# A large attention, pooling and retention kernel: modulation sums, their weight loads and the first operand splits get other places in the plan, and a transpose pair becomes a matmul pair

## The chip, the cores and the metric

The kernel runs on one core of a Trainium2 chip. The metric is the device time of one execution in microseconds (us). Engines are named as in the profile: PE (matmul) with PEld (its weight loads), DVE (vector), ACT (scalar), POOL, and SP, which here only starts transfers.

## The reference

Everything is float32, 512 tokens of width 2048, with 256 context tokens. Three layers follow each other:

```python
# layer 1: attention           layer 2: pooling             layer 3: second block
m = silu(c) @ mod_w + b        # 2048 x 6144; shift, scale, gate (also for c_ctx in layer 1)
h = rmsnorm(x) * (1 + scale) + shift
proj = h @ w_in
y = mix(proj) * silu(z)        # heads 0-7 dense, 8-15 banded | pooling | stick-breaking, retention
x = x + gate * rmsnorm(y @ w_out)      # layer 3 without this norm
```

The "modulation" is the vector-matrix product `silu(c) @ mod_w`. Only its first part in layer 1 (shift and scale, needed for `h` at once) is made in a prologue; the layer-1 gate and all of layers 2 and 3 are made beside the large products.

## The kernel before

**One plan for all engines.** `make_plan` (L311) writes a list of stages. Each engine's program walks through the same list in order and issues its own part of each stage; between engines there are semaphores only. So the place of a stage in the list is its place in the queue of every engine that takes part in it.

**Chunks.** All large weights come in chunks of 512 KB (four 128x256 tiles). SP loads a chunk to one of three RAW buffers (stage `load`, L929, which waits until the buffer's last split is done). Stage `split` makes WHI on ACT (L1129, waits until PE has done with that buffer's chunk of three before) and then WLO = RAW - WHI on DVE (L1484). PE multiplies WHI and WLO with HHI and HLO, the same two-part form of the activations: 24 matmuls of 512 columns for a chunk. `unit` (L349) writes one chunk after the other: the chunk's matmuls in four groups of six with one step of the background tasks after each group, then the splits up to two chunks ahead, then one step of the modulation stream.

**The modulation stream** (`mod_stream`, L428) has 28 jobs of 512 columns, of eight pieces each. A piece is a 512 KB load to one of two MWIDE buffers (`mod_load`, on SP, which waits for the piece two before) and two multiply-adds into MACC on DVE (`mod_acc`). After the eighth piece, `mod_sum` transposes MACC on PE (four 128x128 transposes to the PSUM bank TB) and sums the result on DVE (L1508). PE's next writer of TB waits for that sum. `reduce_pending` is what writes a `mod_sum` to the plan.

**The head phase.** For eight pairs of heads `p`, the loop writes the q product (4 chunks) and the z product (4 chunks); the attention of pair p (`pair_task`, L567) runs in the background from the z product of pair p on, 16 steps there and 16 in the q product of pair p+1. Its first five steps prepare q; event time t = 0 is its sixth step. A head has four query tiles, so a pair has eight, n = 0 to 7: `score` and `softmax` of tile n at t = 3n, `turn` (PE transposes the probabilities through TB, part 0, and OB, part 1) at t = 3n + 4 (3n + 5 for n = 0 and 4), part 1 a step later. The softmax of a tile is one block in DVE's queue: row maximum, then a wait for ACT's exponential, a reciprocal, and the scaling of PB. TB is used by `turn` part 0, `mod_sum` and, for pairs 0 to 3, `q_stat`. Heads 8 to 15 are banded and have two more small mask additions. While a flag `heads` is set, `unit` writes no `mod_sum`; the stream then writes it at its own next step.

**Operand splits of y.** Before the output product of each layer, `first_splits` (L614) writes `y_split` for tiles k = 0 to 11 (HHI on ACT, HLO on DVE) in the last z product, where they take the place of h, so that ACT waits until PE has done with the chunk that used it. Tiles 12 to 15 follow at the end of the last task.

**The prologue** makes 16 rows of layer-1 modulation from 64 loads of 512 KB. `row_cols` (L1909 on PE, L1441 on DVE) turns a 256-wide row ROW into columns: two transposes to TB, a reduction of 16 values to CB, two additions.

Of the kernel before, what the change touches and what calls it, by code (L numbers as in the profile page):

```python
# [11 lines left out]
P = 128  # L12
# [16 lines left out]
         [("od_pool_scale", 0, 16), ("ret_norm_gain_2", 16, 8), ("ev_q_norm", 24, 1), ("ev_k_norm", 25, 1),  # L29
          ("sb_q_gain_2", 26, 1), ("sb_k_gain_2", 27, 1), ("ev_mod_b", 32, 48), ("od_mod_b", 80, 48)],  # L30
         [("b_ada_2", 0, 48)]]
TABLES = ["t_sq", "t_mask", "t_sb", "t_rope_a", "t_rope_b", "t_rcnt", "t_decay"]


class Sig:
# [44 lines left out]
def build(nc, ctx, T, out):  # L80
# [61 lines left out]
    K1 = 1024  # L142
# [6 lines left out]
    MORE = [scratch(f"MORE{i}", [P, 4, 256], F32, 32 * K1 + i * 4 * K1) for i in range(2)]  # L149
    ROW = [scratch(f"ROW{i}", [P, 256], F32, 40 * K1 + i * K1) for i in range(2)]  # L150
    RS = scratch("RS", [P, 32], F32, 44 * K1)
    CB = scratch("CB", [P, 2, 2], F32, 44 * K1 + 128)
    SC32 = scratch("SC32", [P, KT, 32], F32, 42 * K1)
    YSQ = [scratch(f"YSQ{i}", [P, SEQ], F32, 32 * K1 + i * 2 * K1) for i in range(2)]
    XY = [scratch(f"XY{i}", [P, SEQ], F32, 36 * K1 + i * 2 * K1) for i in range(2)]
# [155 lines left out]
    def make_plan():  # L311
# [1 line left out]
        todo = []  # L313
        background = []
        gates = [[], []]
        at = {"load": 0, "split": 0, "use": 0, "unit": 0, "pair": 0, "heads": False}
        scored = []
        summed = set()
        pending = []
# [29 lines left out]
        def unit(work, quiet=False):  # L349
            u = at["unit"]  # L350
            at["unit"] += 1
            n = len(units[u])
            at["pair"] += n // 8 + 1
            for c in range(n):
                i = at["use"]
                at["use"] += 1
                while at["split"] <= i:
                    split_next()
                work(u, i, c, c == n - 1)
                if not at["heads"]:  # L360
                    reduce_pending()
                while at["split"] < min(i + NS, len(chunks)):
                    split_next()
                if not (quiet and c >= n - 2):
                    step([mods])
            return u
# [59 lines left out]
            return unit(work)  # L426

        def mod_stream():  # L428
            for _ in range(4):
                yield  # L430
            put("mod_load", 0)
            put("mod_load", 1)
            yield
            for t in range(len(mod_jobs)):
                for c in range(8):
                    reduce_pending()
                    put("mod_acc", t, c)
                    if 8 * t + c + 2 < 8 * len(mod_jobs):
                        put("mod_load", 8 * t + c + 2)
                    if c < 7:  # L440
                        yield
                pending.append(t)
                yield
            reduce_pending()

        def reduce_pending():
            while pending:
                t = pending.pop()
                put("mod_sum", t)
                summed.add(t)  # L450
# [116 lines left out]
        def pair_task(p):  # L567
            yield
            put("nr_apply", ("q", 2 * p))
            yield  # L570
            if p < 4:
                put("q_stat", p)
            yield
            put("nr_apply", ("q", 2 * p + 1))
            yield
            if p < 4:
                put("q_root", p)
            yield
            events = {}

            def later(t, *stage):
                events.setdefault(t, []).append(stage)

            for n in range(8):
                later(3 * n, "rows", n)
            t = 0
            while events:
                for what, *a in reversed(events.pop(t, [])):
                    if what == "rows":
                        i, qt = divmod(a[0], 4)  # L590
                        h, n = 2 * p + i, 8 * p + a[0]
                        scored.append(n)
                        put("score", h, qt)
                        put("softmax", h, qt, n)
                        two = len(score_jobs(h, qt)[1]) > 4
                        late = 1 if a[0] % 4 == 0 else 0
                        later(t + 4 + late, "turn", h, qt, n, 0, not two)
                        if two:
                            later(t + 5 + late, "turn", h, qt, n, 1, True)
                        if qt == 3:  # L600
                            later(t + 7, "pv", h)
                    elif what == "pv":
                        put("pv", *a)
                        later(t + 1, "gate", *a)
                    else:
                        put(what, *a)
                t += 1
                yield
            if p == 7:
                for k in range(12, KT):  # L610
                    put("y_split", 1, k, h_unit)
                    yield

        def first_splits(layer):  # L614
            for _ in range(4):
                yield
            for k in range(12):
                put("y_split", layer, k, h_unit)
                yield
                if k < 8:  # L620
                    yield

        put("q_scale")
        at["heads"] = True
        task = None
        for p in range(8):
            u, pair = gemm("h", 1)
# [12 lines left out]
        def project_out(layer, h_unit):  # L640
# [14 lines left out]
            for uu in range(2, 8):  # L655
# [3 lines left out]
                else:  # L659
                    background.append(more)  # L660
                u, pair = gemm("y", layer, uu == 7 and layer < 3)
                if layer == 1 and uu < 6:
                    step([mods])
                finish(more)
                for nt in range(2):
                    put("o_copy", layer, 2 * uu + nt, pair, nt, u, (u, nt))
# [34 lines left out]
                put("x_out", q, i)  # L701
                yield

        at["heads"] = False
        need_mods(3)
        put("gate_gain", 1)
        h_unit = project_out(1, h_unit)
# [338 lines left out]
    def act_program(e):  # L1046
# [18 lines left out]
        def rstd(key, stat, n, bank, count):  # L1065
# [6 lines left out]
            af(TY[:, 0:n], TY[:, 0:n], ACT.Exp, 0.0, -0.5).then_inc(*a_rs.up((key, 2)))  # L1072

        e.o.dma_start(SM[0:1, 0:8], T["ev_sink"]).then_inc(*sel.up("sink", by=16))
        e.o.add_instruction(mybir.InstLoadActFuncSet(
            act_func_set_id=NAT_LOG_EXP, name=nc.get_next_instruction_name(),
            engine=mybir.EngineType.Activation, ins=[], outs=[]))
# [298 lines left out]
    def dve_program(e):  # L1376
# [37 lines left out]
        for stage, *a in plan:  # L1414
# [26 lines left out]
            elif stage == "row_cols":  # L1441
                n, = a
                nb = order0[n]
                bias = COL[:, 160 + 2 * nb:162 + 2 * nb]
                e.wait_ge(p_cols, n)
                if n:
                    e.wait_ge(v_cols, (n - 1, "end"))
                e.o.tensor_reduce(CB[:, :, :], TB[:, 0:256].rearrange("p (g j r) -> p g r j", g=2, j=4)[:, :, 0:2, :],
                                  AX_X, ADD).then_inc(*v_cols.up((n, "sums")))
                e.wait_ge(v_cols, (n, "sums"))  # L1450
                tt(MOD[:, 0, 2 * nb:2 * nb + 2], CB[:, :, 0], bias, ADD).then_inc(*v_cols.up((n, 1)))
                tt(MODX[:, 2 * nb:2 * nb + 2], CB[:, :, 1], bias, ADD).then_inc(*v_cols.up((n, 2), (n, "end")))
                if nb >= 8:
                    k = 2 * nb - 16
                    for x, t in enumerate((MOD[:, 0, 16 + k:18 + k], MODX[:, 16 + k:18 + k])):
# [387 lines left out]
    def pe_program(e):  # L1843
# [20 lines left out]

        e.wait_ge(cst, "cst")
        e.wait_ge(par, "par")
        e.wait_ge(sel, "sink")
        for i in range(3):
            tr(TB[:, i * P:(i + 1) * P], PR[:, i, :])
        mm(TB[:, 384:392], ONE[0:1, :], SM[0:1, 0:8], True, True).then_inc(*p_col.up(1))  # L1870
        for stage, *a in plan:
# [37 lines left out]
            elif stage == "row_cols":  # L1909
# [1 line left out]
                e.wait_ge(a_row, n)  # L1911
                e.wait_ge(*tb)
                for nt in range(2):
                    t = tr(TB[:, nt * P:(nt + 1) * P], ROW[n % 2][:, nt * P:(nt + 1) * P])
                t.then_inc(*p_cols.up(n))
                tb = v_cols, (n, "sums")
            elif stage == "kv":
                k, what, part = a
                i = k // 4 * 2 + (0 if what == "k" else 1)
# [310 lines left out]
def tables():  # L2230
# [12 lines left out]
    def rope(ang):  # L2243
# [10 lines left out]
    g = np.log1p(-np.exp2(-5.0 - np.arange(8)))  # L2254
    rel = t[None, :] - i[:, None]
    dec = np.where(rel[None] >= 0, np.exp(np.maximum(rel, 0)[None] * g[:, None, None]), 0.0) * SCALE
    return {"t_sq": sq, "t_mask": mask, "t_sb": sb, "t_rope_a": rope(ang.astype(np.float64)),
            "t_rope_b": rope(ang2.astype(np.float64)), "t_rcnt": rc, "t_decay": dec.astype(f4)}


# [22 lines left out]
```

## Time and profile before

| | |
|---|---|
| three runs | 2639.16, 2639.43, 2641.59 us; median 2639.43 |
| the profiled execution | time 2639.43 us, span 2637.6 us |
| busy | PE 97%, DVE 61%, ACT 36%, POOL 5% of the span |
| mean granted TensorE clock | 0.981 |

The span goes from the first to the last instruction; 1.8 us of the time lie outside it. A busy PE is counted with modelled ends of pipelined matmuls: 512-column matmuls of a chunk start every 0.23 us where the full clock is granted and every 0.43 us where half of it is.

### The profile page before, as it was taken

The page shows a single profiled execution, that of the slowest core. Times are in us where ns is not written, and L with a number is a line of the kernel's source. Part 1 is how long each engine was busy: PE and PEld are TensorE (multiplying, and loading weights), DVE is VectorE, ACT ScalarE, POOL GpSimd, SP SyncE. Part 2 cuts the span into 40 slices and gives each one's busy share as a digit, 9 for nine tenths or more (in the row PEclk, how much of TensorE's full clock was granted, in tenths as well). Part 3 has the DMA queues.
Part 4 walks back from the last instruction along what each step waited for, and adds up shares of the span by engine and source line. Part 5 has one row for each costly group of instructions (what it writes and reads, how often), then busy time and mean ns, then how long its engine had stood idle before and what let it go on. Part 6 is the DMA issues. An engine that isn't in the chain of part 4 may idle for free.

```text
span 2637.6 us, 31436 instructions
## 1 busy us (share of the span) xinstructions
PE 2571.3 (97%) x12691; PEld 2078.8 (79%) x12691; DVE 1608.5 (61%) x2400; ACT 944.1 (36%) x1502; POOL 131.8 (5%) x121
## 2 busy tenths in 40 slices
PE   7999999999999999999999998999999999999998
PEld 4779777777777878888877887787888878878786
DVE  4445666677777768676697757668455534445432
ACT  4222444434444324331334333444344323223321
POOL 0000000000001103001021102000000000000000
PEclk8999999999999989999999998999999999999999
DMA  9934433344447635655657554454222223322432
GB/s 350 341 121 146 128 112 112 112 128 128 128 128 240 207 127 184 202 185 175 212 167 262 178 159 156 143 160 128 80 73 87 86 80 92 92 88 90 155 111 72
DMA packets 301074, 390.67 MB, mean 148 GB/s; under 512 B 11698, under 2 KB 237618, under 8 KB 297090
## 3 DMA queue, kind: packets, MB, share of 16 engines
q1 hardware_dynamic: 294800, 354.79, 42.9%
q0 software_dynamic: 6128, 33.89, 3.4%
q8 instruction: 100, 1.64, 0.3%
q14 instruction: 44, 0.36, 0.0%
q10 hardware_dynamic: 2, 0.00, 0.0%
HBM read 371.85 MB, written 16.78 MB: 147 GB/s over the span
## 4 chain that ended last, share of the span: by engine, by line
PE 87%; DVE 6%; DMA 2%; issue 2%; ACT 2%; SPq 1%; POOL 0%; ACTq 0%; DVEq 0%; POOLq 0%
PE G L1849 72%; PE OB L1849 5%; PE S L1849 5%; PE TB L1849 2%; PE TB L1852 2%; DVE MACC L1387 2%; DMA LATE<-in_ev_mod_w 1%; DMA MRAW<-in_ev_mod_w 1%; DVE WLO L1381 1%; DVE Y L1381 1%; SPq L927 0%; PE OB L1852 0%; DMA MORE<-in_ev_mod_w 0%; DVE SQ L1387 0%; ACT WHI L1056 0%
## 5 line engine op out<-in xcount | busy, mean ns | idle before, releaser
L1849 PE MATMUL G<-HHI,WHI 128*128 128x512 f32 x2624 | 1107.5, 422 | 25.4 <-issue 7.7
L1849 PE MATMUL G<-HHI,WLO 128*128 128x512 f32 x2624 | 1032.9, 394 | 0.0
L1849 PE MATMUL G<-HLO,WHI 128*128 128x512 f32 x2624 | 1030.6, 393 | 0.0
L1381 DVE TENSOR_TENSOR WLO<-RAW,WHI 128x1024 fp32r<-128x1024 f32 x376 | 464.3, 1237 | 331.1 <-ACT WHI L1056 328.2
L1849 PEld LDWEIGHTS G<-HHI,WHI 128*128 128x128 f32 x2624 | 497.3, 190 | 144.4 <-issue 31.5
L1056 ACT ACTIVATE WHI<-RAW 128x1024 fp32r<-128x1024 f32 x376 | 395.7, 1054 | 587.3 <-PE G L1849 534.5
L1849 PEld LDWEIGHTS G<-HLO,WHI 128*128 128x128 f32 x2624 | 498.4, 190 | 113.1 <-issue 17.0
L1849 PEld LDWEIGHTS G<-HHI,WLO 128*128 128x128 f32 x2624 | 496.9, 189 | 109.5
L1387 DVE SCALAR_TENSOR_TENSOR MACC<-MWIDE,SC,MACC 128x512 f32<-128x512 f32 x420 | 340.0, 810 | 23.4 <-DMA MWIDE<-in_w_ada 9.6
L1849 PE MATMUL G<-WHI,HHI 128*128 128x256 f32 x640 | 186.5, 291 | 0.0
L1849 PE MATMUL G<-WLO,HHI 128*128 128x256 f32 x640 | 181.0, 283 | 0.0
L1849 PE MATMUL G<-WHI,HLO 128*128 128x256 f32 x640 | 180.9, 283 | 0.0
L1849 PEld LDWEIGHTS G<-WHI,HHI 128*128 128x128 f32 x640 | 122.5, 191 | 7.7 <-issue 7.0
L1849 PEld LDWEIGHTS G<-WHI,HLO 128*128 128x128 f32 x640 | 122.6, 192 | 2.4 <-issue 1.7
L1849 PEld LDWEIGHTS G<-WLO,HHI 128*128 128x128 f32 x640 | 122.6, 192 | 0.0
L1053 ACT ACTIVATE SQ<-SQ 128x512 f32<-128x512 f32 x144 | 90.8, 631 | 67.9 <-DVE SQ L1387 64.9
L1849 PE MATMUL S<-KTA,QR 128*128 128x256 f32 (+2 forms) x256 | 83.5, 449 | 2.6 <-ACT PB L1198 2.6
L1849 PE MATMUL OB<-PT,VV 128*128 128x512 f32 (+2 forms) x192 | 74.7, 539 | 0.0
L1198 ACT ACTIVATE PB<-S,SM 128x512 f32<-128x512 f32 (+1 forms) x32 | 23.8, 743 | 135.9 <-DVE SM L1384 135.9
L1849 PEld LDWEIGHTS S<-KTA,QR 128*128 128x128 f32 x256 | 47.7, 190 | 29.3 <-issue 15.3
L1198 ACT ACTIVATE PB<-S,SM,COL 128x768 f32<-128x768 f32 x32 | 31.8, 993 | 109.0 <-DVE SM L1384 109.0
L1384 DVE TENSOR_SCALAR TM<-TB 128x512 f32<-128x512 f32 (+1 forms) x28 | 18.8, 673 | 79.6 <-ACT TY L1053 79.4
(270 smaller groups left out, 2367.2 us busy)
## 6 DMA issues: line engine op xcount, KB each, us to landing
RAW<-in_w_in SPq DMA_DIRECT2D x128, 512.0 KB, 3.8
MWIDE<-in_od_mod_w SPq DMA_DIRECT2D x96, 512.0 KB, 4.7
MWIDE<-in_w_ada SPq DMA_DIRECT2D x96, 512.0 KB, 4.6
RAW<-in_ev_w_in SPq DMA_DIRECT2D x80, 512.0 KB, 3.6
RAW<-in_od_w_in SPq DMA_DIRECT2D x64, 512.0 KB, 3.8
MWIDE<-in_ev_mod_w SPq DMA_DIRECT2D x32, 512.0 KB, 4.5
RAW<-in_ev_w_out SPq DMA_DIRECT2D x32, 512.0 KB, 4.1
RAW<-in_od_w_out SPq DMA_DIRECT2D x32, 512.0 KB, 4.0
```

The source lines that it names most:

```text
L1053: return e.o.activation(o, i, fn, bias=bias, scale=scale)
L1056: return e.o.activation(o, i, ACT.Copy, scale=scale)
L1198: e.o.activation(PB[n % 2][:, lo:768], S[:, lo:768], ACT.Exp, bias=nm, scale=1.0 if banded(h) else q_root_of(h, qt), accum_out=SM[:, i + 1 ...
L1381: return e.o.tensor_tensor(o, a, b, op)
L1384: return e.o.tensor_scalar(o, a, s1, s2, op0, op1) if op1 else e.o.tensor_scalar(o, a, s1, None, op0)
L1387: return e.o.scalar_tensor_tensor(out=o, in0=a, scalar=s, in1=b, op0=op0, op1=op1)
L1849: return e.o.matmul(o, l, r, start=start, stop=stop, skip_group_check=True)
L1852: return e.o.transpose(o, i, IDN[:, :])
```

## The change

Four edits in the plan and one in the prologue:

1. The modulation stream has no four empty steps and no pair of loads ahead of it. It writes load n in one step and the multiply-adds of n in the next, so a load stands one chunk ahead of its use instead of two. Four extra steps of the stream in the output product of layer 1 are gone.
2. `unit` writes a pending `mod_sum` after every chunk's matmuls, in the head phase too. `pair_task` may also write it, at event times 3n + 2 for n other than 1 and 5 (2, 8, 11, 14, 20, 23).
3. `first_splits` writes its twelve splits in twelve consecutive steps; before, there was an empty step after each of the first eight.
4. `row_cols` uses two accumulating matmuls of ROW (as weights) with a 128x2 table t_r4 instead of two transposes, and DVE adds the bias straight from TB, without the reduction. TB is handed back after the last DVE operation of the stage and not after the reduction.
5. The table is one more small load from ACT's queue at the start, and PE's first transposes wait for it.

```diff
-        at = {"load": 0, "split": 0, "use": 0, "unit": 0, "pair": 0, "heads": False}
+        at = {"load": 0, "split": 0, "use": 0, "unit": 0, "pair": 0}
...
                 work(u, i, c, c == n - 1)
-                if not at["heads"]:
-                    reduce_pending()
+                reduce_pending()
...
         def mod_stream():
-            for _ in range(4):
-                yield
-            put("mod_load", 0)
-            put("mod_load", 1)
-            yield
             for t in range(len(mod_jobs)):
                 for c in range(8):
+                    put("mod_load", 8 * t + c)
+                    yield
                     reduce_pending()
                     put("mod_acc", t, c)
-                    if 8 * t + c + 2 < 8 * len(mod_jobs):
-                        put("mod_load", 8 * t + c + 2)
-                    if c < 7:
-                        yield
                 pending.append(t)
-                yield
+            yield
             reduce_pending()
...
             for n in range(8):
                 later(3 * n, "rows", n)
+                if n % 4 != 1:
+                    later(3 * n + 2, "sums")
...
+                    elif what == "sums":
+                        reduce_pending()
...
             for k in range(12):
                 put("y_split", layer, k, h_unit)
                 yield
-                if k < 8:
-                    yield
...
-                if layer == 1 and uu < 6:
-                    step([mods])
...
+        e.o.dma_start(SM[:, 40:42], T["t_r4"]).then_inc(*sel.up("r4", by=16))
...
+                v = TB[:, 0:4].rearrange("p (n v) -> p v n", v=2)
-                e.o.tensor_reduce(CB[:, :, :], TB[:, 0:256].rearrange("p (g j r) -> p g r j", g=2, j=4)[:, :, 0:2, :],
-                                  AX_X, ADD).then_inc(*v_cols.up((n, "sums")))
-                e.wait_ge(v_cols, (n, "sums"))
-                tt(MOD[:, 0, 2 * nb:2 * nb + 2], CB[:, :, 0], bias, ADD).then_inc(*v_cols.up((n, 1)))
-                tt(MODX[:, 2 * nb:2 * nb + 2], CB[:, :, 1], bias, ADD).then_inc(*v_cols.up((n, 2), (n, "end")))
+                tt(MOD[:, 0, 2 * nb:2 * nb + 2], v[:, 0, :], bias, ADD).then_inc(*v_cols.up((n, 1)))
+                tt(MODX[:, 2 * nb:2 * nb + 2], v[:, 1, :], bias, ADD).then_inc(*v_cols.up((n, 2), (n, "end")))
...
-        e.wait_ge(sel, "sink")
+        e.wait_ge(sel, "r4")
...
-                    t = tr(TB[:, nt * P:(nt + 1) * P], ROW[n % 2][:, nt * P:(nt + 1) * P])
+                    t = mm(TB[:, 2 * nt:2 * nt + 2], ROW[n % 2][:, nt * P:(nt + 1) * P], SM[:, 40:42],
+                           nt == 0, nt == 1)
                 t.then_inc(*p_cols.up(n))
-                tb = v_cols, (n, "sums")
+                tb = v_cols, (n, "end")
```

## Rows read from the trace of the kernel before

**Rows 1.** The page: busy time of each engine, share, instructions.
```profile
PE 2571.3 (97%) x12691; PEld 2078.8 (79%) x12691; DVE 1608.5 (61%) x2400; ACT 944.1 (36%) x1502; POOL 131.8 (5%) x121
```

**Rows 2.** PE's waits, whole span: releaser, us in total, times, longest.
```profile
PE G L1849 <- DVE HLO L1381: 7.0, 2, 4.0
...
PE G L1849 <- DVE WLO L1381: 4.7, 3, 2.0
```

**Rows 3.** The chain that ended last, 305 to 309 us: start, us, what.
```profile
305.58 1.29 PE S L1849 x4
306.87 1.39 PE G L1849 x6
308.26 0.44 PE TB L1852 x4
```

**Rows 4.** Timeline of DVE, 309 to 312 us: start, us, what.
```profile
309.47 0.62 DVE L1384 TENSOR_SCALAR PB<-PB,SM 128x768 f32<-128x768 f32 x1
310.22 1.23 DVE L1381 TENSOR_TENSOR WLO<-RAW,WHI 128x1024 fp32r<-128x1024 f32 x1
```

**Rows 5.** Timeline of DVE, pair 0.
```profile
270.29 0.68 DVE L1508 TENSOR_REDUCE MOD<-TB 128x4 f32<-128x512 f32 x1
```

**Rows 6.** The chain that ended last, 268 to 274 us.
```profile
268.08 0.44 PE TB L1852 x4
...
273.94 0.44 PE TB L1852 x4
```

**Rows 7.** The chain at a banded pair, first of three.
```profile
591.96 0.43 PE TB L1852 x4
```

**Rows 8.** Timeline of DVE at the same pair.
```profile
594.50 0.55 DVE L1384 TENSOR_SCALAR PB<-PB,SM 128x640 f32<-128x640 f32 x1
```

**Rows 9.** Stretches: us, PE, PEld, DVE, ACT, POOL busy, clock, DMA share, GB/s.
```profile
776.00:780.00 4.00, 3.98 (x14) 2.23 (x14) 3.67 (x6) 2.13 (x4) 0.00 (x0) 1.00 0.00 0
...
793.00:798.00 5.00, 4.55 (x11) 3.58 (x12) 2.96 (x4) 1.10 (x4) 0.00 (x0) 0.50 0.42 116
...
1351.00:1354.50 3.50, 3.49 (x9) 2.71 (x10) 3.43 (x5) 0.00 (x0) 0.00 (x0) 0.52 0.60 164
```

**Rows 10.** Timeline of PE and DVE, last head pair.
```profile
731.21 1.53 DVE L1387 SCALAR_TENSOR_TENSOR MACC<-MWIDE,SC,MACC 128x512 f32<-128x512 f32 x2
...
733.92 1.53 DVE L1387 SCALAR_TENSOR_TENSOR MACC<-MWIDE,SC,MACC 128x512 f32<-128x512 f32 x2
...
775.39 1.34 PE L1849 MATMUL S<-KTA,QR 128*128 128x384 f32 x4 [2.57 <-ACT PB L1198]
...
792.24 0.56 DVE L1384 TENSOR_SCALAR PB<-PB,SM 128x640 f32<-128x640 f32 x1
792.71 0.69 DVE L1381 TENSOR_TENSOR HLO<-Y,HHI 128x512 fp32r<-128x512 f32 x1
...
793.45 0.80 PE L1849 MATMUL G<-HHI,WHI 128*128 128x512 f32 x1 [3.98 <-DVE HLO L1381]
```

**Rows 11.** Timeline of PE and DVE, layer 2.
```profile
1351.01 0.69 PE L1849 MATMUL G<-HHI,WHI 128*128 128x512 f32 x1 [1.96 <-DVE WLO L1381]
...
1353.46 1.53 DVE L1387 SCALAR_TENSOR_TENSOR MACC<-MWIDE,SC,MACC 128x512 f32<-128x512 f32 x2
...
1390.46 0.50 PE L1849 MATMUL G<-PHI,WHI 128*128 128x512 f32 x1 [1.60 <-DVE Y L1387]
```

**Rows 12.** Timeline of SP, the same stretch; the page's DMA issues.
```profile
1350.99 0.37 SPq L933 DMA_DIRECT2D RAW<-in_od_w_in  x1
...
MWIDE<-in_w_ada SPq DMA_DIRECT2D x96, 512.0 KB, 4.6
```

**Rows 13.** Groups of PE by shape: count, busy us, mean ns.
```profile
L1852 PE MATMUL TB<-IDN,ROW 128*128 128x128 f32 x32 | 7.7, 327 | 0.0
...
L1849 PE MATMUL TB<-ONE,TM 128*128 128x1 f32 x32 | 4.1, 250 | 0.0
```

**Rows 14.** A stretch of the prologue, columns as in Rows 9.
```profile
70.00:80.00 10.00, 10.00 (x97) 7.44 (x96) 7.14 (x15) 4.46 (x7) 0.00 (x0) 1.00 1.10 349
```

More of the change, by code:

```diff
@@ L31 @@
          [("b_ada_2", 0, 48)]]
-TABLES = ["t_sq", "t_mask", "t_sb", "t_rope_a", "t_rope_b", "t_rcnt", "t_decay"]
+TABLES = ["t_sq", "t_mask", "t_sb", "t_r4", "t_rope_a", "t_rope_b", "t_rcnt", "t_decay"]
 class Sig:
@@ L151, in build @@
     RS = scratch("RS", [P, 32], F32, 44 * K1)
-    CB = scratch("CB", [P, 2, 2], F32, 44 * K1 + 128)
     SC32 = scratch("SC32", [P, KT, 32], F32, 42 * K1)
@@ L619, in first_splits @@
                 yield
-                if k < 8:
-                    yield
         put("q_scale")
-        at["heads"] = True
         task = None
@@ L702, in write_out @@
                 yield
-        at["heads"] = False
         need_mods(3)
@@ L1443, in dve_program @@
                 nb = order0[n]
+                v = TB[:, 0:4].rearrange("p (n v) -> p v n", v=2)
                 bias = COL[:, 160 + 2 * nb:162 + 2 * nb]
                 e.wait_ge(p_cols, n)
-                if n:
-                    e.wait_ge(v_cols, (n - 1, "end"))
-                e.o.tensor_reduce(CB[:, :, :], TB[:, 0:256].rearrange("p (g j r) -> p g r j", g=2, j=4)[:, :, 0:2, :],
-                                  AX_X, ADD).then_inc(*v_cols.up((n, "sums")))
-                e.wait_ge(v_cols, (n, "sums"))
-                tt(MOD[:, 0, 2 * nb:2 * nb + 2], CB[:, :, 0], bias, ADD).then_inc(*v_cols.up((n, 1)))
-                tt(MODX[:, 2 * nb:2 * nb + 2], CB[:, :, 1], bias, ADD).then_inc(*v_cols.up((n, 2), (n, "end")))
+                tt(MOD[:, 0, 2 * nb:2 * nb + 2], v[:, 0, :], bias, ADD).then_inc(*v_cols.up((n, 1)))
+                tt(MODX[:, 2 * nb:2 * nb + 2], v[:, 1, :], bias, ADD).then_inc(*v_cols.up((n, 2), (n, "end")))
                 if nb >= 8:
@@ L2256, in tables @@
     dec = np.where(rel[None] >= 0, np.exp(np.maximum(rel, 0)[None] * g[:, None, None]), 0.0) * SCALE
-    return {"t_sq": sq, "t_mask": mask, "t_sb": sb, "t_rope_a": rope(ang.astype(np.float64)),
+    r4 = np.stack([i % 32 == 0, i % 32 == 1], axis=1).astype(f4)
+    return {"t_r4": r4, "t_sq": sq, "t_mask": mask, "t_sb": sb, "t_rope_a": rope(ang.astype(np.float64)),
             "t_rope_b": rope(ang2.astype(np.float64)), "t_rcnt": rc, "t_decay": dec.astype(f4)}
```

## The prediction

> **What bounds the kernel now.** I read the page first: PE is busy for 97% of the span, DVE for 61% [rows 1]. Then PE's waits: over the whole span it waits 7.0 us for HLO and 4.7 us for WLO, two of its longest sorts [rows 2]. Then the chain that ended last. In the head phase it consists of PE alone, piece after piece without a hole: six matmuls, a score, six matmuls, four transposes [rows 3, 7]. So there PE sets the time, and every microsecond for which PE must wait for DVE is added to the total, since PE has no idle time in which to win it back. DVE's 61% says nothing about that: what counts is how late DVE's answer comes at the moment PE needs it. Last I read the granted clock around PE's waits: a wait can also be followed by a stretch at the lower of the two levels, 1.2 instead of 2.4 GHz. After the 3.98 us wait the clock is 0.50 for 5 us, after the 1.96 us wait 0.52 for 3.5 us, but after the 2.57 us wait it stays at 1.00 [rows 9 to 11]. Half clock for t us loses t/2: 2.5 and 1.75 us.
>
> **Where mod_sum now falls.** I count plan steps. The stream's calls are: 4 in the first product, 4 in the next, then 8 for each head pair. Before, the first mod_acc is in call 6, so the eighth piece of job t is in call 8t + 13, the first chunk of the z product of pair t. Its mod_sum is written one call later, after background step 8 of pair_task, between t = 2 and t = 3. The trace confirms the count: DVE's sum at 270.29 follows the WLO of that chunk [rows 5].
>
> After the change the first mod_acc is in call 2, so the eighth piece is in call 8t + 9: the first chunk of the q product of pair t, in which the task of pair t-1 makes its steps 17 to 20. Job t is pending after step 20. The event at t = 14 is that very step 20 and comes just too early; the next one is at t = 20, step 26. But unit itself writes the sum after the second chunk, that is after step 24, between t = 18 and t = 19. So the new events in pair_task never find anything, and the sum always stands between the softmax of tile 6 and the turn of tile 5.
>
> **What it costs there, dense pairs.** At t = 18 PE issues the score of tile 6 (305.58), then six matmuls, and at 308.26 it writes TB for tile 5 [rows 3]. With the four transposes of MACC in between (0.44 us, as at 268.08 [rows 6]; they are only moved) it wants TB at 308.70. TB comes free when DVE has summed it. That sum stands in DVE's queue behind the whole softmax of tile 6, whose last operation ends at 309.47 + 0.62 = 310.09 [rows 4]; the sum takes 0.68 [rows 5], so TB is free at about 310.8. PE waits 2.1 us. Before, DVE had the sum done at 270.97 and PE wanted TB at 273.94 [rows 5, 6]: 3.0 us to spare. This arises in the tasks of pairs 0 to 3, jobs 1 to 4: 4 x 2.1 = 8.4 us. Behind the waiting PE stand only its own matmuls, all on the path. The Trainium skill (TensorE: Matmul & The Clock Gate, Architectural detail) says that DVE's queue is strictly first in, first out, so it can't take the sum ahead of the softmax; by a queue that reordered, these waits would be nil, and the trace, with the sum right behind WLO [rows 5], agrees with the page.
>
> **Banded pairs.** The same at 591.96: PE would want TB at 592.40, DVE ends the softmax at 595.05 [rows 7, 8], TB is free at 595.75: 3.4 us. Pairs 4, 5, 6 (jobs 5 to 7), 10.2 us; the other two have the same spacing.
>
> **Clock.** The 3.4 us waits lie between the 1.96 and 3.98 us waits, both of which were followed by half clock: 3 x 2.1 = 6.3 us (bounds 0 and 7.5). The 2.1 us waits lie between 1.96 (half) and 2.57 (none): I take half the chance of 1.75 us each, 3.5 us (bounds 0 and 7).
>
> **The last pair and layer 1's y_split.** Here DVE is already behind: PE waits 2.57 us for the exponential of tile 4, then 3.98 us for HLO of tile 11, which stands right behind the softmax of tile 6 in DVE's queue (792.24, 792.71) [rows 10]. With twelve consecutive steps all splits stand before t = 11. The 3.98 us wait and its 2.5 us of lost clock go away. But five more splits (some 0.6 us of DVE's time each, HLO's row shows 0.69 with its overlap: 3.1 us) now stand ahead of the softmax of tile 4, and the job-7 sum (0.7 us [rows 5]) has left this stretch. At the pair's start the pieces at 731.21 and 733.92 follow each other so closely that the second one's load, issued just before the first and 4.6 us long [rows 12], would come 2.4 us late; an idle time of 0.8 us on DVE takes some of it, 1.6 us stay. So tile 4 comes 4.0 us later, and the 2.57 us wait becomes 6.6. Job 8's sum falls between t = 18 and 19 too: about 2.6 us. Net, with 2.5 us for the clock after the long wait and 1 for the other: 4.0 - 4.0 - 2.5 + 2.6 + 2.5 + 1 = +3.6 us. Bounds: -6.5 (only the gain) to +8.
>
> **Layer 2.** DVE is behind from 1351, where PE waits for WLO, to 1390, where PE waits 1.60 us for silu's last product [rows 11]. Two edits add to that queue. The splits of tiles 8 to 11 move ahead of this silu: 4 x 0.6 = 2.4 us. And the piece at 1353.46 would find its load late: it is issued behind the RAW load at 1350.99, takes 4.6 us [rows 12], and lands at 1356.0, 2.6 us too late; before, it was issued a chunk earlier. DVE has about 1.4 us of idle time to absorb. That makes +3.6, and a possible 1.75 for the clock: I take +4 (bounds 0 and +7).
>
> **Loads one chunk ahead, elsewhere.** A full-speed chunk takes 24 x 0.23 = 5.5 us, a load 4.6. About a third of the pieces, those that DVE runs in quick succession while catching up, would wait 0.3 to 3 us. What hides it is that WLO is made two chunks before PE needs it; PE's three WLO waits sum to 4.7 us now [rows 2], in DVE's worst stretches. I take +1 for these and for layer 3's denser splits together (bounds 0 and +6). The four early pieces of the stream and the four removed extra steps cancel: at the end of layer 1's output product both versions have 101 pieces done, and from there the phases are the same. On SP the new order lets no RAW load wait longer.
>
> **Prologue.** A 128-wide transpose pair costs little: 32 records take 7.7 us. A one-column float32 matmul shows as two records (32 of them, 4.1 us, for 16 matmuls), 0.26 us for each matmul [rows 13]; a two-column one is nearest to that, and 32 of them make 8.2 us. By the spacing in the chain, 0.11 us for a transpose [rows 3], it would be 4.7 us more. Both lie under the loads, which run at 349 GB/s and a share of 1.10 with PE just busy [rows 14]. DVE saves a reduction per row, of use only at the last one. I take 0 (bounds -1 and +4.7). The later release of TB meets nobody: its next user is the next row. The table's load is issued ahead of the one that PE's first transposes wait for anyway: 0.
>
> **Sum.** 8.4 + 3.5 + 10.2 + 6.3 + 3.6 + 4 + 1 + 0 = 37.0 us. The profiled execution took 2639.43 us, which is the median of the three runs: 2676.4 us, I say 2676.
>
> **Rivals.**
> - *The waits come, but without their clock losses, and the last pair gains.* 8.4 + 10.2 and little else: 2655 to 2662. For it: the 2.57 us wait that cost no clock [rows 9, 10]. Chance 0.2. The Trainium skill (TensorE: Matmul & The Clock Gate, HAM oscillation) holds that waits between bursts of matmuls can bring the half clock back each time. [...]
> - *Late loads decide.* If DVE's third of late pieces meets less slack than I take, PE waits for WLO in layers 1 and 2 as it now does at 1351 [rows 11]: ten such places at 1.96 + 1.75 would make another 37 us: 2700 and more. Against it: only three such waits exist now. Chance 0.07.
> - *Faster.* The place is y_split: PE's wait for HLO in layer 1 (3.98 plus 2.5 of clock) goes, and mod_sum causes no waits because I have miscounted its step by three or more (at t = 14 to 16, say, before a turn with spare time). Then -6.5 plus layer 2's 0 to 4: about 2634. It decides if the sums' seven waits together are under 6 us. Against it: the count reproduces the place before. Chance 0.05.
> - *No change that can be told.* The sum misplaced as above and the y_split edit neutral: 2639. Chance 0.06.
>
> **Chances.** My forecast, all terms, 0.62; the rivals 0.2, 0.07, 0.05, 0.06. Adding the bounds that can fall together (no clock losses and +12 at the low end; all clock losses, +8 and +7 at the high end: 8.4 + 7 + 10.2 + 7.5 + 8 + 7 + 4 = 52), the range is 2652 to 2692. A measurement of this kernel tells about 0.2% (5 us) from no change: slower 0.89, same 0.06, faster 0.05.
>
> **What the profile of the changed kernel would show.** PE's waits get a row TB <- DVE MOD (L1508's line) with seven or eight entries, 2 us in four and 3.4 us in three. The four transposes of MACC stand after the score of tile 6. The 3.98 us wait for HLO in the last pair is gone and the one for PB there is longer. DVE's idle time before MACC, ended by MWIDE, has several times the entries. Half-clock stretches follow the 3.4 us waits. In the prologue rows for CB are missing. It would prove me wrong if PE still showed no wait for MOD, or if TB's wait were under 1 us because DVE takes the softmax of tile 6 sooner than in rows 4.

## The result and the profile after

| | before | after |
|---|---|---|
| median | 2639.3 us (4 runs, 2636.88 to 2641.59) | 2684.93 us (4 runs, 2680.59 to 2688.49) |
| profiled execution | 2639.43 us, span 2637.6 | 2682.9 us, span 2681.1 |
| mean granted clock | 0.981 | 0.979 |

The changed kernel is slower by 1.7%, clear of the noise: ratio 1.0172, 95% interval 1.0154 to 1.0191. The forecast was 2676 us with a range of 2652 to 2692. The two profiled spans differ by 43.5 us, and the time is divided with these two executions.

The page after, busy time of each engine, its share of the span and its instructions:

```profile
PE 2585.2 (96%) x12723; PEld 2087.5 (78%) x12723; DVE 1609.1 (60%) x2384; ACT 945.0 (35%) x1502; POOL 135.6 (5%) x121
```

Set against [rows 1], this page says almost nothing: a point less for PE. PE's waits after (releaser, us in total, times, longest) say more:

```profile
PE TB L1838 <- DVE MOD L1494: 21.5, 8, 3.4
...
PE G L1835 <- DVE WLO L1371: 9.5, 6, 4.0
...
PE S L1835 <- ACT PB L1188: 6.0, 3, 2.5
PE G L1835 <- DVE HLO L1371: 5.4, 3, 3.1
...
PE TB L1838 <- DVE MACC L1377: 2.3, 2, 1.7
```

The first row is new, and the one for WLO has doubled against [rows 2]. The chain that ended last, at the place of [rows 3], shows what the first row is:

```profile
304.62 1.39 PE G L1835 x6
306.01 0.22 PE OB L1838 x2
306.23 1.31 PE S L1835 x4
...
307.56 0.97 DVE SM L1568
...
310.12 0.62 DVE PB L1374
310.74 0.61 DVE MOD L1494
...
311.48 0.63 PE TB L1838 x4
```

Before, the chain there was PE alone. Now it leaves PE after the score, goes through DVE's softmax and the sum behind it, and comes back to PE only with the transposes of tile 5.

To see where the rest went I read the start of the same ACT evictions (copies of a finished product out of PSUM) in both timelines: the first of a pair's q product ("q copy"), the first of a layer's output product ("output copy"), and the ninth of the upward product in layer 2's pooling ("upward tile 8"). How much later each one comes (drift), and the same for the experiments' profiled executions, stands in this table; time before in the first column, drifts in us:

| landmark | before | after | a1 | b1 | a2 | a3 | b2 | b3 |
|---|---|---|---|---|---|---|---|---|
| first q copy | 251.3 | +1.1 | +2.3 | -0.3 | +1.2 | +3.2 | +0.2 | +1.6 |
| q copy of pair 7 | 732.6 | +28.4 | +3.8 | +26.6 | +28.0 | +30.1 | +0.2 | +3.6 |
| layer 1, first output copy | 829.5 | +32.3 | +2.7 | +27.6 | +29.3 | +32.9 | -2.9 | +5.3 |
| layer 2, upward tile 8 | 1194.5 | +34.8 | +12.9 | +29.5 | +31.7 | +34.0 | -1.8 | +15.3 |
| layer 2, first output copy | 1433.9 | +47.5 | +27.5 | +29.4 | +34.4 | +47.5 | +0.9 | +30.9 |
| end of the span | 2637.6 | +43.5 | +24.0 | +25.1 | +30.4 | +45.8 | -3.2 | +27.7 |

(a1: the phase put back. b1: the phase alone. a2: loads two chunks ahead again. a3: old spacing of the splits again. b2: dense splits alone. b3: loads one chunk ahead alone.)

In the changed kernel the eight drifts at the q copies are +1.1, 3.4, 5.7, 8.0, 11.8, 17.0, 23.3 and 28.4: steps of 2.3, 2.3, 2.3 and 3.9 us for the dense pairs, 5.2, 6.3 and 5.2 for the banded ones, where the waits are 2.13 and 3.41 us. Then come 3.9 us in the last pair, 2.5 to the upward tile and 12.6 to layer 2's first output copy.

The 4 us by which the drift falls after that (47.5 to 43.5) are no gain of the change. The runs b1, b4 and c1 leave layer 3 as it was (but for b1's earlier stream), and their drifts fall as well: by 4.3, by 4.2 (-0.1 to -4.2) and by 3.2 us (-1.7 to -4.9). The profiled execution of the kernel before was itself late there, at two places. One (2.3 us against b4) is a 1.95 us wait for HLO at 1596 us with a granted clock of 0.66 behind it, where b4 waits 1.56 us and keeps 1.00. The other (1.8 us) is half clock after a 3.06 us wait that b4 and the changed kernel have too, at full clock. PE's timeline and a window behind the wait, first before, then changed:

```profile
2475.21 0.76 PE L1849 MATMUL G<-HHI,WHI 128*128 128x512 f32 x1 [3.06 <-DVE HLO L1381]
2475.20:2480.20 5.00, 4.99 (x12) 3.94 (x13) 3.94 (x5) 0.88 (x1) 1.89 (x4) 0.50 0.78 282
```

```profile
2520.53 0.47 PE L1835 MATMUL G<-HHI,WHI 128*128 128x512 f32 x1 [3.06 <-DVE HLO L1371]
2520.50:2525.50 5.00, 4.34 (x18) 3.30 (x19) 3.96 (x5) 0.90 (x1) 1.91 (x4) 1.00 0.80 279
```

So the change costs 47.5 us by these two executions, and the medians, 45.6 us apart, agree better with that than the spans do.

### The profile page after: what moved, and what is told of

Its sections match the earlier page's. It is cut to its first block, busy times and chain, and to the rows that moved or that the text cites. A ratio compares the mean times of both kernels' runs of the same rounds, so it can differ in the third digit from the quotient of the medians.

```text
span 2681.1 us, 31475 instructions
## 1 busy us (share of the span) xinstructions
PE 2585.2 (96%) x12723; PEld 2087.5 (78%) x12723; DVE 1609.1 (60%) x2384; ACT 945.0 (35%) x1502; POOL 135.6 (5%) x121
## 4 chain that ended last, share of the span: by engine, by line
PE 80%; DVE 9%; DMA 4%; ACT 3%; issue 3%; SPq 1%; POOL 0%; DVEq 0%; ACTq 0%; POOLq 0%
PE G L1835 66%; PE S L1835 5%; PE OB L1835 5%; DVE MACC L1377 2%; PE TB L1835 2%; DMA MWIDE<-in_w_ada 2%; PE TB L1838 1%; DMA MRAW<-in_ev_mod_w 1%; DVE WLO L1371 1%; DVE SM L1568 1%; DMA MWIDE<-in_od_mod_w 1%; ACT PB L1188 1%; ACT WHI L1045 1%; DVE Y L1371 1%; DVE SQ L1377 1%
## 5 line engine op out<-in xcount | busy, mean ns | idle before, releaser
L1835 PEld LDWEIGHTS S<-KTA,QR 128*128 128x128 f32 x256 | 47.4, 189 | 33.0 <-issue 15.3
L1568 DVE TENSOR_REDUCE SM<-S 128x1 f32<-128x768 f32 (+2 forms) x64 | 54.8, 855 | 25.4 <-PE S L1835 23.8
```

What stands on the lines that cost most here:

```text
L1568: e.o.tensor_reduce(nm, S[:, lo:768], AX_X, MAX, negate=True).then_inc(*v_sm.up((h, qt, "row")))
L1835: return e.o.matmul(o, l, r, start=start, stop=stop, skip_group_check=True)
```

## The experiments

Each ratio is to the kernel before on the same chip: median 2635.14 us for a1, b1, a2 and a3, 2637.43 for b3, b2, a4 and a5, and 2637.74 for a6, c1, c2 and b4.

### Phase of the stream put back (a1)

```diff
         def mod_stream():
+            for _ in range(4):
+                yield
             for t in range(len(mod_jobs)):
...
+                if layer == 1 and uu < 6:
+                    step([mods])
                 finish(more)
```

> The changed kernel with only the phase of the modulation stream put back: four empty steps at its start and the four extra steps in layer 1's output product; loads still one chunk ahead, mod_sum still written by unit after each chunk, splits dense. My theory: the phase alone puts mod_sum behind the softmax of tile 6, so PE's waits for MOD (21.5 us in eight) vanish, and with them 27 us in pairs 0 to 6 (10.7 + 16.6 of drift) and the sum's share of the last pair (about 2.8 us): 2653 to 2659 us. Layer 2's drift of some 12 us stays. Rival: DVE is late in the pairs because of late loads or dense splits, and the place only shows it: PE's waits stay in some form and the time is 2675 or more.

Measured: 2664.63 us, ratio 1.0108 [1.0094, 1.0121], +29 us. In the waits of PE the row for MOD is gone; these stand in its place (columns as above):

```profile
PE G L1839 <- DVE WLO L1375: 11.7, 7, 4.2
...
PE TB L1842 <- DVE MACC L1381: 6.3, 6, 2.4
```

The drift stays at +2.3 us through six of the eight q copies and is 2.5 and 3.8 us at the last two. So the phase alone put the sum where it hurts, and the new rule in `unit` is harmless without it. But the total missed the expectation by 6 to 12 us: with the old phase the late loads cost more than in the changed kernel, 10.2 us between layer 1's first output copy and the upward tile (2.5 there), and 14.6 in layer 2 (12.6 there).

### Phase moved alone (b1)

```diff
         def mod_stream():
-            for _ in range(4):
-                yield
             put("mod_load", 0)
...
-                if not at["heads"]:
-                    reduce_pending()
+                reduce_pending()
...
-                if layer == 1 and uu < 6:
-                    step([mods])
```

> The kernel before with only the phase moved (no empty steps, no extra steps) and mod_sum written after each chunk's matmuls; loads still two chunks ahead, splits sparse, transposes in the prologue. My theory: the waits for MOD appear as in the changed kernel, 2.1 us in four pairs and 3.4 in three, +27 us over pairs 0 to 6, +3 in the last pair, layer 2 about as before: 2666 to 2671 us. Rival: the waits need the late loads too: under 2650 us.

Measured: 2665.77 us, ratio 1.0113 [1.0100, 1.0127], +31 us, at the lower edge of what was expected. The waits for MOD are there with loads two chunks ahead:

```profile
PE TB L1847 <- DVE MOD L1503: 23.3, 8, 4.6
```

Layer 2 has no drift (29.5 to 29.4). The late loads have no part in the pairs.

### Loads two chunks ahead again (a2)

```diff
+            put("mod_load", 0)
+            put("mod_load", 1)
+            yield
...
-                    put("mod_load", 8 * t + c)
-                    yield
                     reduce_pending()
                     put("mod_acc", t, c)
+                    if 8 * t + c + 2 < 8 * len(mod_jobs):
+                        put("mod_load", 8 * t + c + 2)
+                    if c < 7:
+                        yield
                 pending.append(t)
-            yield
+                yield
```

> The changed kernel with only the loads of the modulation stream two chunks ahead again, everything else (phase, sums, dense splits) as changed. DVE's order is the same, only SP's differs. My theory: layer 2's excess (+12.7 us where I had forecast +4) and the 2 to 3 us in layer 1's output product come from late loads: both go, 2669 to 2674 us, and PE's waits for MOD are unchanged. Rival: the twelve dense splits or the phase itself cost this in layer 2: 2683 to 2687 us.

Measured: 2671.86 us, ratio 1.0135 [1.0121, 1.0149], +37 us, as expected. DVE's order is that of the changed kernel, so the difference is the loads alone. DVE's groups for MACC (count, busy us, mean ns, idle before them and what ended it), first of the changed kernel and then of this one:

```profile
L1377 DVE SCALAR_TENSOR_TENSOR MACC<-MWIDE,SC,MACC 128x512 f32<-128x512 f32 x420 | 341.2, 812 | 126.4 <-DMA MWIDE<-in_w_ada 58.9 <-DMA MWIDE<-in_od_mod_w 50.7 <-DMA MWIDE<-in_ev_mod_w 8.4
```

```profile
L1382 DVE SCALAR_TENSOR_TENSOR MACC<-MWIDE,SC,MACC 128x512 f32<-128x512 f32 x420 | 336.5, 801 | 24.7 <-DMA MWIDE<-in_w_ada 8.7 <-DMA MWIDE<-in_od_mod_w 7.4 <-DMA MWIDE<-in_ev_mod_w 0.6
```

The late loads give DVE 102 us more of idle time, and the total only 13 us more (10 by the ratios, which compare within a chip). Most of it is slack. Where it is not, is seen in layer 2. The changed kernel, timelines of DVE and of PE:

```profile
1365.24 1.54 DVE L1377 SCALAR_TENSOR_TENSOR MACC<-MWIDE,SC,MACC 128x512 f32<-128x512 f32 x2 [2.93 <-DMA MWIDE<-in_w_ada]
...
1375.14 8.47 DVE L1377 SCALAR_TENSOR_TENSOR MACC<-MWIDE,SC,MACC 128x512 f32<-128x512 f32 x2
1383.54 5.71 DVE L1371 TENSOR_TENSOR WLO<-RAW,WHI 128x1024 fp32r<-128x1024 f32 x1
...
1389.31 0.79 PE L1835 MATMUL G<-HHI,WHI 128*128 128x512 f32 x1 [4.00 <-DVE WLO L1371]
```

The same work with loads two ahead:

```profile
1357.68 1.53 DVE L1382 SCALAR_TENSOR_TENSOR MACC<-MWIDE,SC,MACC 128x512 f32<-128x512 f32 x2
...
1368.49 8.47 DVE L1382 SCALAR_TENSOR_TENSOR MACC<-MWIDE,SC,MACC 128x512 f32<-128x512 f32 x2
1376.89 5.76 DVE L1376 TENSOR_TENSOR WLO<-RAW,WHI 128x1024 fp32r<-128x1024 f32 x1
...
1382.71 0.79 PE L1840 MATMUL G<-HHI,WHI 128*128 128x512 f32 x1 [1.96 <-DVE WLO L1376]
```

A single late load (2.93 us) shortly before DVE's slow stretch makes PE's wait there 4.00 instead of 1.96 us. The pair of multiply-adds that usually takes 1.53 us takes 8.47 there in both kernels, while POOL is busy as well (8.24 of those 8.40 us in the changed kernel; no run separates the two), and DVE has no idle time in it. One part of the theory holds only in part: layer 1's output product keeps its drift in a2 (29.3 to 29.2 at 904 us), but 2.5 us arise behind it, at the start of layer 2, where PE waits 2.34 us for HLO, then at half clock, against 1.56 and full clock before. b2 and c1, with loads as before, show the same there (2.37 and 2.47 us), so it is not the loads.

### Old spacing of the first splits (a3)

```diff
                 put("y_split", layer, k, h_unit)
                 yield
+                if k < 8:
+                    yield
```

> The changed kernel with only the old spacing of the first splits (an empty step after each of the first eight). My theory: layer 2's excess stays, the last pair gets its 4 us wait for HLO back but loses the longer wait for the exponential: 2682 to 2689 us. Rival: the dense splits are what costs 12.7 us in layer 2: 2671 to 2675 us.

Measured: 2685.21 us, ratio 1.0187 [1.0173, 1.0202]; as expected, the splits are not what costs time in layer 2 (drift 34.0 to 47.5, as in the changed kernel). The part on the last pair missed: no wait for HLO came back. PE waits 2.56 us for the exponential and then 4.97 us for MOD.

### One chunk ahead alone (b3)

```diff
-            put("mod_load", 0)
-            put("mod_load", 1)
-            yield
...
+                    put("mod_load", 8 * t + c)
+                    yield
                     reduce_pending()
                     put("mod_acc", t, c)
-                    if 8 * t + c + 2 < 8 * len(mod_jobs):
-                        put("mod_load", 8 * t + c + 2)
```

> The kernel before with only the loads of the modulation stream one chunk ahead instead of two; phase, place of mod_sum, splits and prologue as before. DVE's order is that of before. My theory, from the run with only the phase put back (+24 us, of which 8 in layer 1's output product and 14.6 in the first part of layer 2): late loads alone cost that, 2655 to 2661 us, nothing in pairs 0 to 6, and PE's waits for WLO grow from 3 to about 7. Rival: late loads do harm only together with the dense splits, since each alone is covered by DVE's slack: 2645 us or less.

Measured: 2667.23 us, ratio 1.0122 [1.0104, 1.0140], +30 us: the rival is out, and the theory was 6 us short again. Here the loads alone cost as much as the phase alone: 10.0 us between layer 1's first output copy and the upward tile, 15.6 in layer 2. One place stands out in layer 1's output product. Timelines of SP, DVE and PE:

```profile
863.94 0.37 SPq L928 DMA_DIRECT2D RAW<-in_ev_w_out  x1
864.35 1.41 SPq L936 DMA_DIRECT2D MWIDE<-in_od_mod_w  x2
...
863.84 1.53 DVE L1382 SCALAR_TENSOR_TENSOR MACC<-MWIDE,SC,MACC 128x512 f32<-128x512 f32 x2
869.44 1.54 DVE L1382 SCALAR_TENSOR_TENSOR MACC<-MWIDE,SC,MACC 128x512 f32<-128x512 f32 x2 [4.07 <-DMA MWIDE<-in_od_mod_w]
...
871.03 1.11 PE L1847 MATMUL TB<-IDN,MACC 128*128 128x128 f32 x4 [5.49 <-DVE MACC L1382]
```

This is one of the four extra steps of the stream: two loads are issued at once, the piece of the second is wanted at once, and it is the last of its job, so PE's transposes stand behind it. The drift rises by 7.7 us there. How much one such place costs depends on how near behind PE is: a1 has the same stream and waits only 0.83 us for MACC at this one, but loses 10.2 us over the same stretch, in several places. The changed kernel has no extra steps any more and loses 2.5 us there, so it is spared some 8 us of what its own late loads would cost: the two parts of its first edit, later loads and no extra steps, partly hide each other. The four edits measured alone sum to 30.6 + 29.8 + 0.9 + 3.3 = 64.6 us (the medians of b1, b3, b2 and b4 less those of the kernel before), all together make 45.6. Some 8 of the 19 us between them are this; the rest was not traced.

### Dense splits alone (b2), and in layer 1 only (c1)

```diff
                 put("y_split", layer, k, h_unit)
                 yield
-                if k < 8:
+                if k < 8 and layer > 1:
                     yield
```

(The diff is c1's; b2 has no empty step in any layer.)

> The kernel before with only the first twelve splits in consecutive steps. My theory: in the last head pair the 3.98 us wait for HLO goes and the wait for the exponential of tile 4 (2.57 us) grows by some 3 us, -1 to -3 us; in layer 2, where DVE is behind as well, +0 to +3 us: 2634 to 2641 us. Rival: the wait for the exponential grows as much as the one for HLO shrinks and half clock follows it, and layer 2 pays for four splits: 2643 us or more.

> The kernel before with the first twelve splits in consecutive steps in layer 1 only; layers 2 and 3 keep the old spacing. From the run with dense splits in all layers: -3.1 us in the last head pair, +2.7 in layer 2. My theory: the two are independent, so the gain stays and the loss goes: 2632 to 2635 us, faster than the kernel before by 0.1 to 0.2%. Rival: the loss in layer 2 is a shift of DVE's order that comes with the earlier last pair too: no difference.

Measured: b2 2638.29 us, ratio 1.0003 [0.9994, 1.0012]; c1 2635.47 us, ratio 0.9992 [0.9983, 1.0001]. c1 lies 0.5 us above its range. In the profiles the last pair gains 3.1 and 3.2 us in both. Layer 2 loses 2.6 us in b2, but 1.4 in c1 too, where nothing was changed in it, so about half of b2's loss can't be laid to the splits. The totals can't be told from no change, c1's 2.3 us only nearly. PE's timeline of b2 in the last pair:

```profile
770.07 1.13 PE L1847 MATMUL S<-KTA,QR 128*128 128x256 f32 x4 [1.49 <-ACT PB L1196]
778.26 1.65 PE L1847 MATMUL S<-KTA,QR 128*128 128x384 f32 x4 [2.48 <-ACT PB L1196]
```

The 3.98 us wait for HLO of [rows 10] is gone; the wait for the exponential of tile 4 has not grown (2.48 against 2.57), but a second one, a tile earlier, has joined it, and one of 0.83 us for tile 1.

### The prologue's matmuls: undone (a4) and alone (b4)

```diff
-                    t = mm(TB[:, 2 * nt:2 * nt + 2], ROW[n % 2][:, nt * P:(nt + 1) * P], SM[:, 40:42],
-                           nt == 0, nt == 1)
+                    t = tr(TB[:, nt * P:(nt + 1) * P], ROW[n % 2][:, nt * P:(nt + 1) * P])
```

(a4, with the reduction and without the table's load; b4 is the reverse on the kernel before.)

> The changed kernel with only the prologue's row_cols as before (two transposes, the reduction to CB, no table load). My theory: the two-column matmuls cost PE up to 2 us in the prologue (q0's drift of 1.1 us, which the run with row_cols as before and the phase moved doesn't show): 2683 to 2685 us, q0 at 250.5 to 251.5 us. Rival: the prologue is set by its loads and differs by chance: no difference to the changed kernel.

> The kernel before with only row_cols as changed: two accumulating matmuls with the table, the bias straight from TB, and the table's load. My theory: it lies under the prologue's loads: within 1.5 us of the kernel before at the first q product and at the end. Rival: the matmuls are float32 ones that cost PE 4.7 us in the prologue, all on the path: 2640 to 2643 us.

Measured: a4 2689.65 us, ratio 1.0201 [1.0187, 1.0215]; b4 2641.04 us, ratio 1.0012 [1.0003, 1.0021]. Both expectations for the total missed. a4 is slower than the changed kernel's 1.0172 rather than faster, and its first q copy drifts by 2.4 us, not less than 1.1. b4's median is 3.3 us up, inside the range of the rival that the matmuls lie on the path, but its profiled execution, its fastest, is at +0.9 at the first q copy, as the theory has it. b4's group of PE (count, busy us, mean ns):

```profile
L1845 PE MATMUL TB<-SM,ROW 128*128 128x2 f32 x64 | 10.8, 274 | 0.0
```

64 records for 32 matmuls, 10.8 us of PE where the transposes took 7.7 [rows 13]; the prediction had 8.2 by the one-column rows. With drifts of -1.2 (c1) to +4.1 us (c2) at the first q copy over these executions, and each sign of the edit measured slower, whether it costs 0 or 3 us stays open.

### The sum ahead of the softmax of tile 5 (a5)

```diff
                         put("score", h, qt)
+                        if a[0] == 5:
+                            reduce_pending()
                         put("softmax", h, qt, n)
```

> The changed kernel with one more place where a pending mod_sum is written: in the head pairs, between the score and the softmax of tile 5 (event time 15), four steps ahead of where it now falls and ahead of that tile's softmax in DVE's queue. Phase, loads and splits as changed. My theory: PE's waits for MOD came from DVE's queue (the sum behind the softmax of tile 6), so they vanish without moving the phase: about 27 us less in the pairs 0 to 6 and 1 to 3 in the last, 2654 to 2661 us. Rival: the sum needs MACC's last piece, which DVE has only just made there, and TB is wanted two steps later: waits for MACC or MOD of 1 to 2 us stay in each pair, 2668 us or more.

Measured: 2689.02 us, ratio 1.0196 [1.0182, 1.0210]. My theory fell, the rival held. DVE's and PE's timelines:

```profile
298.30 1.53 DVE L1379 SCALAR_TENSOR_TENSOR MACC<-MWIDE,SC,MACC 128x512 f32<-128x512 f32 x2
...
299.89 1.11 PE L1840 MATMUL TB<-IDN,MACC 128*128 128x128 f32 x4 [2.11 <-DVE MACC L1379]
```

The sum is out of the softmax's shadow, but PE gets to the transposes before the last piece is in MACC: 27.7 us of waits for MACC, in eleven, in place of 21.5 for MOD. Eight of them stand at this place, 2.11 us in the dense pairs and 3.64 in the banded ones:

```profile
PE TB L1840 <- DVE MACC L1379: 27.7, 11, 3.6
```

### The sum ahead of pv (a6), and with two more repairs (c2)

```diff
                     elif what == "pv":
+                        reduce_pending()
                         put("pv", *a)
```

(c2 has also a2's stream and c1's splits.)

> The changed kernel with one more place where a pending mod_sum is written: at t = 16, ahead of the first head's pv. In the run with the place at t = 15 PE waited 2.1 us for MACC instead of for MOD: the transposes stood 2.1 us too early. One group of six matmuls later (1.4 us) MACC is 0.7 us late, and TB's next user is only behind pv. My theory: the wait needs a place that is late enough for MACC and at least two steps ahead of TB's next user; here PE's waits for MACC are 0.5 to 0.8 us a pair, those for MOD nil, and 18 to 26 us go: 2658 to 2666 us. Rival: DVE comes to the sum only behind the softmax of tile 5 and the silu product behind it, and the wait for MOD returns: 2675 us or more.

> The changed kernel with three repairs: loads two chunks ahead, a pending mod_sum also written at t = 16 ahead of pv, and the dense splits in layer 1 only. The new phase and the prologue's matmuls stay. My theory: the three causes found (place of the sum, late loads, layer 2's splits) are all there is: 2637 to 2645 us, of which up to 5 for MACC's lateness in the pairs. Rival: the phase has a cost of its own beside the place of the sum: 2650 us or more.

Measured: a6 2724.1 us, ratio 1.0329 [1.0315, 1.0343]; c2 2709.12 us, ratio 1.0274 [1.0260, 1.0288]. Both theories missed by far; the rivals' bounds hold, but by another mechanism. Timelines of PE and DVE in a6:

```profile
300.06 0.66 PE L1839 MATMUL TB<-IDN,MACC 128*128 128x128 f32 x4 [0.73 <-DVE MACC L1378]
305.42 7.07 PE L1836 MATMUL OB<-PT,VV 128*128 128x512 f32 x12 [4.71 <-DVE MOD L1495]
...
302.46 0.62 DVE L1375 TENSOR_SCALAR PB<-PB,SM 128x768 f32<-128x768 f32 x1
304.07 0.69 DVE L1378 SCALAR_TENSOR_TENSOR SQ<-G,SQ 128x512 f32<-128x512 f32 x1 [0.99 <-ACT SQ L1043]
304.68 0.68 DVE L1495 TENSOR_REDUCE MOD<-TB 128x4 f32<-128x512 f32 x1
```

In the dense pairs the wait for MACC is the 0.73 us I had worked out; in the banded ones it is 2.26, not 0.5 to 0.8. What I had not counted is that `pv` also waits for TB: PE's code has it wait for the last user of TB, since the probabilities come from there by way of ACT. I had put the sum directly ahead of that wait, and DVE reaches it behind a softmax and a silu product. This costs 4.71 us (5.23 in the banded pairs) and then lost clock in the long pv (granted clock 0.50 to 0.74 in the 5 us behind the waits), together 7.3 to 10.7 us a pair by the drift of the q copies. c2 thus tested this mistake a second time; it shows only that its two other repairs are worth 15 us together. Whether a place exists at which the new phase costs nothing was not found out.

## Why the prediction was right, and where it was off

**Place of the sum: right.** After step 24, between t = 18 and t = 19. The four dense waits were forecast as 2.1 us and are 2.13; the three banded ones as 3.4 and are 3.41. a1 (away without the phase) and b1 (there with the phase and the new rule in `unit`, without late loads or dense splits) show the cause. My words "behind the softmax of tile 6 in DVE's queue" hold for the place, but a5 and a6 show that they are half of it: a place must also be late enough for MACC and far enough ahead of TB's next waiter, and neither of the two tried is both.

**Clock of the pairs: the sum right, its division nearly.** Windows of the changed kernel (us, busy of PE, PEld, DVE, ACT and POOL, clock, DMA share, GB/s), behind a 2.13 us wait, behind another one, and behind a 3.41 us wait:

```profile
312.00:317.00 5.00, 5.00 (x24) 3.76 (x23) 2.38 (x4) 0.99 (x2) 0.00 (x0) 1.00 0.61 208
536.00:541.00 5.00, 5.00 (x19) 3.81 (x18) 1.83 (x3) 0.99 (x2) 0.00 (x0) 0.70 0.60 207
607.50:612.50 5.00, 5.00 (x18) 4.01 (x18) 1.97 (x3) 0.94 (x3) 0.00 (x0) 0.68 0.53 141
```

For the dense pairs I took 3.5 us, and one wait in four was paid, with some 1.6. For the banded ones I took 6.3, and their drift of 16.6 us less 10.2 of waits leaves 6.4. The rival without clock losses is out by that. The Trainium skill (TensorE: Matmul & The Clock Gate, HAM oscillation) says that waits between bursts of matmuls can bring the half clock back each time. The trace has it both ways: four of the seven waits did, three did not. Which of the four dense ones is paid differs from run to run, so the half chance was a fair price but each single case is luck.

**Last pair: the sum right (+3.9 for +3.6) by luck, its parts not.** The wait for HLO went. But the wait for the exponential did not become 6.6 us: the changed kernel shows 1.50 and 2.46 us, b2 1.49 and 2.48. I had put the time of all five splits on tile 4; by b2's rows an earlier tile takes part of it. What filled the sum instead are a 2.04 us wait for the exponential earlier in the pair (0.78 with loads two ahead, in a2, so a late load takes part in it) and 2.78 us for job 8's sum (forecast 2.6).

**Layer 2: the term that was under-sized.** I took +4 us with bounds of 0 and +7; the drift is 12.6, of which 10 are the loads (a2 keeps 2.7 in layer 2). The mechanism, a late piece behind a RAW load in DVE's worst stretch, is the one forecast. What failed is the step "DVE has about 1.4 us of idle time to absorb" for one piece: the late pieces follow one another, and PE waits at four more places after the first, for MACC (1.66 us), WLO (0.67), silu's product (3.13 against 1.60) and HLO (1.7).

**Loads elsewhere: +2.5 us for +1, and small only for a reason I had not seen.** I wrote that the early pieces and the removed extra steps cancel. They cancel in count. In time the removal saves what b3 and a1 show, some 8 us in layer 1's output product. What is left there comes from one very late piece (10.24 us, last section).

**Prologue and table: 0 forecast, +1.1 at the first q copy**, within the spread of these executions.

By the drifts the terms then read 10.7 + 16.6 for the pairs, 3.9 for the last pair, 12.6 for layer 2, 2.5 for loads elsewhere and 1.1 for the prologue: 47.4 us for the 37.0 of the forecast. Layer 2 alone is 8.6 us of that excess, and is about the size of the miss in the total (2684.93 for 2676). That the spans differ by only 43.5 us is the late execution before, not a term of mine.

## What to carry to other kernels

Where one engine sets the time and two others work through lists in a fixed order, the phase of a background task against the foreground is a parameter in itself: four empty steps (with the rule in `unit`) were worth 27 us in seven pairs, and two other places for the displaced stage did not win them back. Before a stage that borrows a shared buffer is moved, list every waiter on that buffer, the indirect ones too; a6 came out 39 us slower than the changed kernel, mostly by one that I had not listed. And edits that seem independent may be covering each other, so each is best run alone and taken away alone: here 65 us of parts made 46 us.

## What the runs showed of the hardware

- **The same wait is followed by half clock in one execution and not in another.** In five kernels (the changed one, a2, a3, a4, b1) PE waits for MOD at the same eight places. Of the twenty waits of 2.12 or 2.13 us six were followed by matmuls 0.43 us apart instead of 0.23, and which ones differs from kernel to kernel; of the fifteen of 3.39 to 3.42 us all were, and so were the five of 2.78 to 4.97 us. At this place a wait of 2 us costs some 1.6 us more in three cases of ten, one of 3.4 us costs 1.5 to 2.9 more each time. But length alone does not decide it: a 3.06 us wait for HLO late in layer 3 stands in all fourteen profiles of this case, and half clock follows it in six (the kernel before, a1, a4, a5, a6 and c2: granted clock 0.50 to 0.74 in the next 5 us) and not in the other eight (1.00, the changed kernel among them). What else decides it stays open. One such difference is worth as much as a small edit here.
- **A load can be late by far more than its usual time.** After the heads, while POOL's queue also loads x back, one piece of the changed kernel came 10.24 us after DVE was ready for it, where the loads' median before was 4.6 us [rows 12]. WLO of that chunk stood behind it in DVE's queue, and PE waited 1.82 us for it, then ran at a granted clock of 0.66 for 5 us: the drift rises by 3.2 us there (31.4 to 34.6), which a2, with loads two chunks ahead, does not show. Timelines of DVE and PE:

```profile
861.86 1.54 DVE L1377 SCALAR_TENSOR_TENSOR MACC<-MWIDE,SC,MACC 128x512 f32<-128x512 f32 x2 [10.24 <-DMA MWIDE<-in_od_mod_w]
...
865.67 0.50 PE L1835 MATMUL G<-HHI,WHI 128*128 128x512 f32 x1 [1.82 <-DVE WLO L1371]
```
